# A two-layer mixer block and a hybrid layer on one core: SBUF tensors begin at multiples of 128 bytes

## What is computed

```python
h = h + dilated_attention_mixer(rms_norm(h, ..), a_w_in, ..)   # 16 heads, three dilations, rope
h = h + swiglu(rms_norm(h, ..), w_gate_up[0], w_down[0])       # hidden 2816
h = h + gla_mixer(rms_norm(h, ..), b_w_in, w_gate_f, w_gate_b, ..)  # gated linear attention, 4 heads
h = h + swiglu(rms_norm(h, ..), w_gate_up[1], w_down[1])
# third layer: modulated by silu(c) @ w_mod; latent attention beside a gated delta rule
x = x + g1 * merge_branches(latent_attention(..), gdn_output(gdn_bidirectional(..)), gates, ..)
x = x + g2 * conv_ffn(modulate(rms_norm(x), sh2, sc2), w_up, conv_w, conv_b, w_down)
return rms_norm(x, final_norm_w)
```

## Time and profile before

| | |
|---|---|
| runs | 1730.6, 1731.4, 1733.53 us; median 1731.4 us |
| span of the profiled execution | 1731.7 us, 0.3 us over the median of the runs; no other time is given for it |
| TensorE matmuls | busy 95% of the span, 10084 |
| weight loads | busy 82%, 10084 |
| VectorE, ScalarE, GpSimd | busy 66%, 47%, 17% |
| mean granted TensorE clock | 0.992 of full speed |
| moved by DMA | 241 MB, mean 139 GB/s |

### The profile page before, as it was taken

One profiled execution on the slowest core, in us unless ns is written; L12 is line 12 of the kernel. 1 busy time (PEld: TensorE's weight loads), 2 busy tenths in 40 slices (PEclk: granted clock), 3 DMA queues, 4 the chain that ended last, 5 costly groups with the idle time before them and its releaser, 6 DMA issues. The chain is left out here.

```text
span 1731.7 us, 25073 instructions
## 1 busy us (share of the span) xinstructions
PE 1637.8 (95%) x10084; PEld 1417.3 (82%) x10084; DVE 1151.1 (66%) x1576; ACT 810.7 (47%) x1034; POOL 290.7 (17%) x239
## 2 busy tenths in 40 slices
PE   8999999899999989999999899989899999999997
PEld 7878888799987866899887688659698978889986
DVE  6776766488885656676457754368887555667764
ACT  5436554544433553544444344465444554356542
POOL 4643330000010010000006200047645000000000
PEclk9999999999999999999999999999999999999999
DMA  7544331387784531786454042000000255545543
GB/s 265 189 153 146 122 122 49 98 268 258 244 304 135 170 121 48 247 289 196 156 183 134 17 125 74 0 19 1 1 2 13 68 193 183 178 158 172 183 169 110
DMA packets 155394, 240.96 MB, mean 139 GB/s; under 512 B 12272, under 2 KB 80624, under 8 KB 155152
## 3 DMA queue, kind: packets, MB, share of 16 engines
q1 hardware_dynamic: 141632, 208.69, 36.8%
q0 software_dynamic: 6816, 27.08, 4.4%
q10 hardware_dynamic: 6832, 3.59, 0.8%
HBM read 238.29 MB, written 1.05 MB: 138 GB/s over the span
## 5 line engine op out<-in xcount | busy, mean ns | idle before, releaser
L196 DVE TENSOR_TENSOR wlo<-raw,whi 128x2048 fp32r<-128x2048 f32 x200 | 460.4, 2319 | 195.0 <-ACT whi L190 194.7
L190 ACT ACTIVATE whi<-raw 128x2048 fp32r<-128x2048 f32 x200 | 375.3, 1886 | 276.8 <-PE ps L326 194.6
L324 PE MATMUL ps<-xs,whi 128*128 128x256 f32 (+1 forms) x1312 | 382.8, 292 | 9.9 <-DVE wlo L196 6.4
L325 PE MATMUL ps<-xs,whi 128*128 128x256 f32 (+1 forms) x1312 | 380.9, 290 | 0.0
L326 PE MATMUL ps<-xs,wlo 128*128 128x256 f32 (+1 forms) x1312 | 380.8, 290 | 0.0
L324 PE MATMUL ps<-whi,xs 128*128 128x512 f32 x672 | 269.7, 401 | 9.8 <-DVE wlo L196 6.4
L326 PE MATMUL ps<-whi,xs 128*128 128x512 f32 x672 | 264.9, 394 | 0.0
L324 PEld LDWEIGHTS ps<-xs,whi 128*128 128x128 f32 x1312 | 247.8, 189 | 20.8 <-issue 14.3
L325 PE MATMUL ps<-wlo,xs 128*128 128x512 f32 x672 | 263.3, 392 | 0.0
L326 PEld LDWEIGHTS ps<-xs,wlo 128*128 128x128 f32 x1312 | 247.3, 188 | 5.8
L325 PEld LDWEIGHTS ps<-xs,whi 128*128 128x128 f32 x1312 | 246.8, 188 | 5.7
(11 more groups left out here) (361 smaller groups left out, 2370.7 us busy)
## 6 DMA issues: line engine op xcount, KB each, us to landing
raw<-in_ffn_w_gate_up SPq DMA_DIRECT2D x88, 512.0 KB, 5.0
raw<-in_a_w_in SPq DMA_DIRECT2D x72, 512.0 KB, 4.5
raw<-in_w_in SPq DMA_DIRECT2D x60, 512.0 KB, 4.6
wide<-in_w_mod POOLq DMA_DIRECT2D x24, 1024.0 KB, 6.8
raw<-in_w_up SPq DMA_DIRECT2D x44, 512.0 KB, 4.7
raw<-in_ffn_w_down SPq DMA_DIRECT2D x40, 512.0 KB, 4.6
raw<-in_b_w_in SPq DMA_DIRECT2D x24, 512.0 KB, 4.6
raw<-in_w_down SPq DMA_DIRECT2D x20, 512.0 KB, 4.2
```

Of the source, the lines that this page charges most:

```text
L190: self.hi_ok.inc(act.activation(self.whi[:, h % NHI, 0:nk, :], self.raw[:, h % NRAW, 0:nk, :], ACT.Copy))
L196: self.lo_ok.inc(dve.tensor_tensor(self.wlo[:, h % NRAW, 0:nk, :], self.raw[:, h % NRAW, 0:nk, :], self.whi[:, h % NHI, 0:nk, :].bitcast(F ...
L324: pe.matmul(o, ahi, bhi, start=start, stop=False)
L325: pe.matmul(o, ahi, blo, start=False, stop=False)
```

## The change

Three roundings become coarser: the start of the first tensor, the size of each placed tensor, and the length of the arena are now multiples of 128 bytes (32 words) where they were of 64 bytes, 8 words and 8 words.

```diff
@@ def build @@
-    at = [nc.sbuf_base + (-nc.sbuf_base) % 64]
+    at = [nc.sbuf_base + (-nc.sbuf_base) % 128]
 
     def place(name, shape, dt=F32, offset=None):
         n = int(np.prod(shape[1:]))
         t = nc.alloc_sbuf_tensor_at(name, shape, dt, offset=at[0] if offset is None else offset)
         if offset is None:
-            at[0] += 4 * (n + -n % 8)
+            at[0] += 4 * (n + -n % 32)
         return t
...
     xs = place("xs", [P, 4, KT, SEQ], F32R)
     arena_at = at[0]
-    arena_n = (nc.sbuf_usable_end - arena_at) // 4 // 8 * 8
+    arena_n = (nc.sbuf_usable_end - arena_at) // 4 // 32 * 32
```

## The result

The changed kernel takes 1738.93 us (median of 12 runs, 1736.93 to 1740.91) where the kernel before takes 1731.26 us beside it (12 runs). The ratio is 1.0038, with an interval of 1.0028 to 1.0049: slower, by 6.6 us going by the ratio. The forecast was 1726, so its sign is wrong. Of the rivals only C had the kernel slower, at 1749.

The account below looks back on a forecast made before the run. TensorE, busy 95% of the span in a chain of matmuls, was taken as the bound; gains of 4.2 us (hid) and 1.5 us (double columns) made 5.7 us off 1731.7, so 1726, range 1708 to 1739.

Parts of the forecast that it names:

- C: Rival, chance 0.17: distance between the two operands' offsets matters, so beginning together slows up-projections 6.6 us, by-token 10.7; 1749 us.
- What bounds the kernel: Whole program: a chain of matmuls, TensorE busy 95% of the span, its pace being what changed addresses can touch.
- each ns counts once: Down-projection stages: TensorE sets their time, so each ns saved per matmul counts in full; gain 4.2 us.
- hid: Stationary operand of 792 down-projection matmuls, offset 96 to 0: 5.3 ns less each, 4.2 us gained; bounds 0 to 5.6.
- Double columns: 384 matmuls with xs moving in twice 256 columns, offset 64 to 0: 4.0 ns each, 1.5 us gained.
- 256 columns: Matmuls with xs moving in 256 columns: taken as 0; bounds 8.7 us gained to 6.6 us lost.
- By token: 2016 matmuls with xs stationary, offset 64 to 0: taken as 0; bounds 3.6 us gained to 10.7 us lost.
- The float32 work, ScalarE, VectorE and DMA at 0: TensorE's float32 work, the other engines' writes and the transfers: offsets cost nothing, 0 us.
- Rival A: Chance 0.22: both operands at 0 suit the reads; short pace in all up-projections, 227.0 ns elsewhere, 20.1 us gained, 1711.
- Rival B: Chance 0.20: nothing changes, hid being slow for its place in SBUF or row order; time stays 1731.
- The 16-byte rule: SBUF is read in 16-byte lines; all starts are multiples of 32 bytes, so no read changes: 0 instead of 5.7 us.

Follow-up runs that it names:

- e3: The changed kernel with everything moved by 128 bytes (hid 128 back), keeping all distances between tensors: 1739.99 us, ratio 1.0027 to the kernel before.
- e2: The changed kernel with xs and the arena 128 bytes further, so xs, hid and weights all begin at 128 modulo 256: 1730.86 us, ratio 0.9979.
- e1: The kernel before with hid moved 96 bytes lower, the tile ending at hid moving along: 1728.55 us, ratio 0.9974 to the kernel before.
- e5: The changed kernel with xs at 192 and hid at 64 modulo 256, weights at 128: 1732.40 us, beside the kernel before at 1734.6.
- e6: The changed kernel with xs at 32 and hid at 192 modulo 256, weights at 128: 1742.86 us, beside the kernel before at 1734.6.
- e9: e2 with xs under a second name, 64 bytes lower, where it feeds a feed-forward: 1722.06 us, ratio 0.9937 to the kernel before.
- e8: The changed kernel with xs at 160 and hid at 32 modulo 256, weights at 128: 1740.73 us, beside the kernel before at 1734.6.

## Why the prediction was wrong, step by step

- **What bounds the kernel: right.** TensorE's spacing, at a granted clock of 1.00 (the 2.4 GHz level) in every stretch quoted, changed the time. But "each ns counts once", said of hid, held only in part: 5.6 us of spacing were 4.6 in the total there, and over all kinds 11.0 us of spacing came to 4.2.
- **hid, forecast 4.2 us of gain at 228.8 ns: right in sign, undersized, for a wrong reason.** It came to 227.1 ns, my far bound, 5.6 us. I had taken "an offset of 0 is no worse than the 64 of xs". The offset is not what did it: the change put hid at distance 0 from the weights, and at its own start of 0 modulo 256 (e3) or 128 (after) it takes the same time.
- **Double columns, forecast 1.5 us of gain: 0.3 us.** I costed their place with the by-token row, 228.8 ns; D went from 64 to 128, 233.3 to 232.4 ns.
- **256 columns, taken as 0: the step that failed most.** The argument was that two paces at one offset mean that the offset does not choose. It doesn't choose between the two, but it does choose whether there are two. Measured 3.0 ns x 3552 = 10.6 us by spacing, 6.9 us with the waits counted. My bound, "all long, 6.6 us", was too small since the new pace (118.7) is above the long one of before (117.8).
- **By token, taken as 0: the second that failed.** D went from 192, one of the two good distances, to 128: 3.1 ns x 2016 = 6.3 us by spacing, 3.3 in the total.
- **The float32 work, ScalarE, VectorE and DMA at 0: right.** The float32 total fell by 1.0 us, VectorE's and ScalarE's busy times moved by 1.6 and 0.1. L764 and L800 take 632 and 693 ns as in the earlier trace rows, the loads of transposes 143 and 141 ns as in the earlier trace rows, and the stream on cst 5.32 us as in the earlier trace rows.
- **Rival C, chance 0.17: its first step was the right one, its geometry wrong.** Distance counts, as it said, but modulo 256 and not 128, and beginning together (D = 0) is the best place for 512 columns, not the worst. What I held against it, "64 apart gives 228.8 and 232.8 ns", falls away once the distance has a sign: those were D = 192 and D = 64. Its price, 17.3 us, is close to the 16.9 us of spacing that these two kinds cost, but by luck: it had 6.6 us for the 256-column kind and 10.7 by token, and they cost 10.6 and 6.3. That loads and moving reads meet in one place, its reason, was not tested. It gave 1749 since it let hid gain nothing, and since no wait was let shrink.
- **Rival A fell with the changed kernel**, where both operands begin at 0 modulo 128 and only the down-projections reach 227 ns; e2 and e3 show that where the operands begin does not matter by itself. **Rival B fell with e1**, where hid's pace follows its start alone. The 16-byte rule of the Trainium skill (SBUF — State Buffer, Specifications) foresaw no change for any of these starts; the traces show 227.0 to 234.2 ns among starts that are all multiples of 32, so the rule doesn't cover this cost and the measurement decides.
- The range, 1708 to 1739, held the time, barely, thanks to the bounds and not to the forecast.

What a reader could have seen in the rows of before: four spacings and three tensors are enough to write down each pair's distance, and I wrote down offsets modulo 128 because that was the unit of the change. The rows would have shown that hid and xs as stationary tiles differ in distance too; which distances are good they could not show.

**Left open.** Why the distance matters was not tried by itself. The load of the next stationary tile runs beside the moving reads, and the pattern would fit reads of the two that meet in the same part of memory; that is argued, not shown. Why the 256-column kind picks one of two paces at D = 64 after a restart of the stream is open too. So are the 3.0 to 5.1 us by which the total of the float32 work was shorter in e2, e5, e6 and e9 than in the kernel before. e5 to e8 have one run each; their spacings are means over hundreds of matmuls, their times are single.

## What to carry to other kernels

Aligning tensors did not of itself make TensorE faster here; what could be had was the distance between the stationary and the moving tensor's starts, modulo 256 here. Measure the spacing of each kind of matmul in a gap-free stretch, one byte offset at a time, since kinds with 512 and with 256 columns liked different distances, and a tensor that serves both can be given two names. And count a change of pace through the waits: in the stages where the weights came late, part of a loss or a gain was absorbed there.

## What was not expected of the hardware

- With 512 moving columns in fp32r and a load of 128 columns before each matmul, the spacing is between 227.0 and 234.2 ns by D alone, a spread of 3.2% at a granted clock of 1.00. It was the same at DMA shares of 0.38 and 0.42 (227.1 and 227.0 ns in the changed kernel).
- With 256 columns the best case for 512 is the worst: 119.9 ns at D = 0, and 113.3 ns, 5.5% less, only in parts of streams at D = 64 or 192.
- The listed duration follows the spacing: 389 ns at D = 0, 395 at D = 128, 396 to 397 at D = 96, and for 256 columns 276 to 283 ns.
